# One two-block transformer kernel, one core: the first dense product begun between two halves of the transposes, and four other steps in other places

## The reference, cut to what matters

```python
# block 1
h = rmsnorm(x) ; u = h @ w_in            # ax az bq bk bv bz cq ck cv cz and gate logits
ya = pool_mixer(ax) * silu(az) ; yb = windowed_attention(bq, bk, bv) * silu(bz)
yc = causal_attention(cq, ck, cv) * silu(cz)
merged = sigmoid(g0)*(ya@wa) + sigmoid(g1)*(yb@wb) + sigmoid(g2)*(yc@wc)
x = rmsnorm(x + merged @ w_out)
# block 2
mod = silu(c) @ ada_w + ada_b            # shift1 scale1 gate1 shift2 scale2 gate2
h = rmsnorm(x)*(1+scale1) + shift1 ; proj = h @ w_in_2   # qa ka va fa qb kb vb, gates
merged = sigmoid(ga)*(forgetting_attention @ wf) + sigmoid(gb)*(stick_breaking_attention @ ws)
x = x + gate1 * (merged @ w_out_2)
y = 16 experts, top 2 of the top group   # gate, up and down matrices, 96 MB in all
x = rmsnorm(x + gate2 * y)
```

## Time and profile before

| | |
|---|---|
| runs | 710.71, 711.07, 711.32 us |
| profiled execution | 710.51 us, span 708.7 us |
| PE busy | 684.0 us (97%) |
| DVE busy | 451.4 us (64%) |
| ACT busy | 325.6 us (46%) |
| POOL busy | 2.6 us |
| DMA | 201.65 MB, mean 285 GB/s |

### The profile page before, as it was taken

One profiled execution on the slowest core, in us unless ns is written; L12 is line 12 of the kernel. 1 busy time (PEld: TensorE's weight loads), 2 busy tenths in 40 slices (PEclk: granted clock), 3 DMA queues, 4 the chain that ended last, 5 costly groups with the idle time before them and its releaser, 6 DMA issues.

```text
span 708.7 us, 9990 instructions
## 1 busy us (share of the span) xinstructions
PE 684.0 (97%) x3846; PEld 481.6 (68%) x3846; DVE 451.4 (64%) x820; ACT 325.6 (46%) x538; POOL 2.6 (0%) x5
## 2 busy tenths in 40 slices
PE   9999999999999998999999989999999999999894
PEld 4999999777788776999877658864343344343342
DVE  6578967877968888587987668675323423422425
ACT  6644444746676647333567766332213213212214
POOL 1000000000000000000000000000000000000000
PEclk9999999999999998999999999999999999999999
DMA  8977777554466432677847553687999999999961
GB/s 349 421 279 304 295 270 305 209 198 135 163 244 231 179 133 105 236 266 314 327 163 283 221 208 119 238 332 291 420 425 423 428 427 426 422 429 423 419 259 59
DMA packets 20011, 201.65 MB, mean 285 GB/s; under 512 B 2434, under 2 KB 3458, under 8 KB 7556
## 3 DMA queue, kind: packets, MB, share of 16 engines
q1 hardware_dynamic: 19248, 200.08, 71.1%
q10 hardware_dynamic: 724, 1.04, 0.5%
HBM read 200.07 MB, written 1.05 MB: 284 GB/s over the span
## 4 chain that ended last, share of the span: by engine, by line
PE 89%; ACT 3%; DMA 3%; DVE 2%; issue 2%; ACTq 0%; DVEq 0%
PE psum L911 18%; PE psum L912 17%; PE psum L913 17%; PE psum L1270 14%; PE psum L1318 8%; DMA ring<-in_expert_w_down 3%; PE psum L1235 3%; PE psum L1215 2%; PE psum L1167 2%; PE psum L1133 1%; PE psum L1113 1%; PE psum L1151 1%; ACT ring_rounded L1517 1%; DVE ring_rounded L1905 1%; PE psum L1136 1%
## 5 line engine op out<-in xcount | busy, mean ns | idle before, releaser
L1905 DVE TENSOR_TENSOR ring_rounded<-ring,ring_rounded 128x1024 fp32r<-128x1024 f32 (+1 forms) x131 | 154.2, 1212 | 29.0 <-ACT ring_rounded L1517 28.9
L1517 ACT ACTIVATE ring_rounded<-ring 128x1024 fp32r<-128x1024 f32 (+1 forms) x132 | 130.5, 1037 | 9.6 <-PE psum L913 6.8
L911 PE MATMUL psum<-hT_rounded,ring_rounded 128*128 128x256 f32 x360 | 102.5, 285 | 0.4 <-ACT foxT L1448 0.4
L913 PE MATMUL psum<-hT_rounded,ring_rounded 128*128 128x256 f32 x360 | 101.9, 283 | 0.0
L912 PE MATMUL psum<-work_rounded,ring_rounded 128*128 128x256 f32 x360 | 101.9, 283 | 0.0
L912 PE MATMUL psum<-ring_rounded,hT_rounded 128*128 128x512 f32 (+1 forms) x224 | 86.6, 386 | 0.0
L1270 PE MATMUL psum<-ring,work 128*64 128x512 f32 x320 | 83.8, 592 | 0.4 <-issue 0.4
L911 PE MATMUL psum<-ring_rounded,hT_rounded 128*128 128x512 f32 (+1 forms) x208 | 83.7, 402 | 0.0
L913 PE MATMUL psum<-ring_rounded,work_rounded 128*128 128x512 f32 (+1 forms) x208 | 80.0, 385 | 0.0
L911 PEld LDWEIGHTS psum<-hT_rounded,ring_rounded 128*128 128x128 f32 x360 | 69.1, 192 | 1.1 <-ACT foxT L1448 0.6
L912 PEld LDWEIGHTS psum<-work_rounded,ring_rounded 128*128 128x128 f32 x360 | 69.1, 192 | 0.1
(11 more groups left out here) (304 smaller groups left out, 1079.8 us busy)
## 6 DMA issues: line engine op xcount, KB each, us to landing
ring<-in_chunks SPq DMA_DIRECT2D x44, 2048.0 KB, 8.2
ring<-in_expert_w_down SPq DMA_DIRECT2D x16, 2048.0 KB, 16.2
ring<-in_expert_w_gate SPq DMA_DIRECT2D x12, 2048.0 KB, 15.1
ring<-in_expert_w_up SPq DMA_DIRECT2D x8, 2048.0 KB, 18.1
gates<-in_expert_w_up SPq DMA_DIRECT2D x8, 1024.0 KB, 21.0
hT<-in_expert_w_gate SPq DMA_DIRECT2D x4, 1024.0 KB, 15.7
mixed<-in_expert_w_gate SPq DMA_DIRECT2D x4, 1024.0 KB, 17.7
ring<-in_chunks SPq DMA_DIRECT2D x4, 512.0 KB, 7.8
```

The source lines that it names most:

```text
L911: nc.tensor.matmul(out, a[0], b[0], start=start, stop=False, skip_group_check=True)
L913: return nc.tensor.matmul(out, a[1], b[0], start=False, stop=stop, skip_group_check=True)
L1517: nc.scalar.activation(as_rounded(high_piece(c, q)), src[:, piece_of(c, q)], ACT.Copy).then_inc(chunk_hi, 1)
L1905: v.tensor_tensor(as_rounded(w[:, piece]), w[:, piece], was_rounded(high_piece(c, q)), ALU.subtract)\
```

## The change

Five groups of edits, all of them to the order of steps.

1. Start. `scale 0 1` and the last two pieces of `cv` go ahead of the second pair of `hT` units, the third piece's low part goes from POOL to DVE, and the first half of `tm cv 0` is begun on PE ahead of that pair. The `keep_busy` calls around the `hT` units fall from 2, 2, 1 and 2 to 1, 1, none and none.
2. Output product of block 1: the low parts of pieces 2 and 3 of `wout 1 1` go ahead of unit `mT 1 1 1`.
3. Second norm of block 2's input: pieces 2 and 3 of `vb` are split behind the norm steps, not ahead of them.
4. Block 2: `mod 4` and `mod 5` go from behind `FT` to right behind `fa` and `logf`; `sigmoid 0` goes from behind `tm h1 1` to behind `tm h2 0` and its heads.
5. Around `proj f`: the low part of its piece 1 goes ahead of the begin of `tm h3 1`; `gate_cols 1`, `mod 10` and `mod 11` go from around `proj s 0 0` to right behind the low parts of pieces 2 and 3, ahead of `proj f 0 0`.

```diff
@@ -50,7 +50,6 @@
 SPLIT = 4
 POOL_FROM = 4
 FIRST = ("cv",)
-FIRST_ON_POOL = 2
 ROAMING = ("va",)
 PLACED = (FIRST, ROAMING, ("proj", "b"), ("proj", "f"), ("proj", "s"), ("vb",), ("qa",), ("wout", 1, 0), ("wout", 1, 1), ("wout", 2, 1))
 PIECES = (0, 1, 2, 3)
@@ -148,15 +147,16 @@
         if low_on_dve(FIRST, q):
             steps.append(("split_low", FIRST, q))
 
-    steps += [("norm", 0, 0), ("norm", 0, 1), ("scale", 0, 0), ("scale", 0, 1)]
+    steps += [("norm", 0, 0), ("norm", 0, 1), ("scale", 0, 0)]
     split_first(0)
     unit("hT", 0, 0, 0)
     unit("hT", 0, 0, 1)
     split_first(1)
+    steps += [("begin", "tm", "cv", 0), ("scale", 0, 1)]
+    split_first(2)
+    split_first(3)
     unit("hT", 0, 1, 0)
     unit("hT", 0, 1, 1)
-    split_first(2)
-    split_first(3)
     unit("tm", "cv", 0)
     unit("tm", "cv", 1)
     for name in ("cz", "bz", "az", "ax", "cq", "ck"):
@@ -227,8 +227,8 @@
         split_placed(two, (0, 1, 2, 3), (0, 1))
         unit("wout", 1, 0, 0)
         steps.append(("norm_half", 1, 0))
+        split_placed(two, (), (2, 3))
         unit("mT", 1, 1, 1)
-        split_placed(two, (), (2, 3))
         split_placed(va, (2, 3), (0,))
         unit("wout", 1, 0, 1)
 
@@ -242,11 +242,12 @@
     unit("hT", 1, 0, 1)
     steps.append(("norm_half", 1, 1))
     split_placed(va, (), (2, 3))
-    split_placed(vb, (0, 1, 2, 3))
+    split_placed(vb, (0, 1))
     unit("wout", 1, 1, 1)
     steps.append(("norm", 1, 1))
     split_placed(vb, (), (0,))
     steps.append(("norm", 2, 1))
+    split_placed(vb, (2, 3))
 
     unit("tm", "va", 0)
     split_placed(vb, (), (1, 2, 3))
@@ -264,11 +265,11 @@
     steps.append(("gate_cols", 0))
     unit("fa",)
     steps.append(("logf",))
+    unit("mod", 4)
+    unit("mod", 5)
     unit("fm", "qb", 0)
     some_ada(2)
     unit("FT",)
-    unit("mod", 4)
-    unit("mod", 5)
     todo = pairs_of_heads(8)
     seq = [(("fm", "qb", 1), 1), (("fm", "kb", 0), 1), (("fm", "kb", 1), 2), (("tm", "h0", 0), 1),
            (("tm", "h0", 1), 2), (("tm", "h1", 0), 1), (("tm", "h1", 1), 2), (("tm", "h2", 0), 1),
@@ -279,9 +280,10 @@
         if u == ("tm", "h3", 1):
             split_placed(f, (), (0,))
             steps.append(("y_split_low", "f"))
+            split_placed(f, (), (1,))
         unit_and_heads(u, n)
         some_ada(ADA_HERE.get(u[1:], 0))
-        if u == ("tm", "h1", 1):
+        if u == ("tm", "h2", 0):
             steps.append(("sigmoid", 0))
         if u == ("tm", "h2", 1):
             steps.append(("y_split", "f"))
@@ -289,7 +291,10 @@
         if u == ("tm", "h3", 0):
             split_placed(f, (2, 3))
         if u == ("tm", "h3", 1):
-            split_placed(f, (), (1, 2, 3))
+            split_placed(f, (), (2, 3))
+            steps.append(("gate_cols", 1))
+            unit("mod", 10)
+            unit("mod", 11)
             split_placed(sb, (0, 1))
         if u == ("proj", "f", 0, 0):
             split_placed(sb, (2, 3), (0,))
@@ -300,10 +305,8 @@
             steps.append(("y_split_low", "s"))
             split_placed(sb, (), (2, 3))
     assert not todo
-    steps += [("sigmoid", 8), ("mods", 1), ("gate_cols", 1)]
+    steps += [("sigmoid", 8), ("mods", 1)]
     unit("proj", "s", 0, 0)
-    unit("mod", 10)
-    unit("mod", 11)
     unit("proj", "s", 0, 1)
     unit("mT", 2, 0, 0)
     unit("proj", "s", 1, 0)
@@ -387,7 +390,7 @@
 
 def low_on_dve(c, q):
 
-    return q != FIRST_ON_POOL if c == FIRST else q < POOL_FROM
+    return c == FIRST or q < POOL_FROM
 
 
 def chunk_of(step):
@@ -409,6 +412,7 @@
 
 STEPS, CHUNKS = plan()
 UNITS = [s[1:] for s in STEPS if s[0] == "unit"]
+BEGUN = [s[1:] for s in STEPS if s[0] == "begin"]
 SILU = ("cz", "bz", "az")
 ADA_ORDER = [s[1:] for s in STEPS if s[0] == "ada"]
 
@@ -1180,8 +1184,7 @@
                 last = nc.tensor.matmul(bank[4 + half], one_row[32 * half:32 * half + 1, :], norm_row[half],
                                         start=True, stop=True)
             last.then_inc(norm_rows_ready, 1)
-            keep_busy(2)
-            n, begun = 0, False
+            keep_busy(1)
             for s in STEPS:
                 if s[0] == "residual":
                     if s[1] == 0:
@@ -1191,15 +1194,13 @@
                     pe.wait_ge(*evicted(("wout", 2, s[1] // 2, 1)))
                     residual(s[1]).then_inc(residual_done, 1)
                 if s[0] == "begin":
-                    unit(n, s[1:], (0,))
-                    begun = True
+                    unit(UNITS.index(s[1:]), s[1:], (0,))
                 elif s[0] == "unit":
                     if s[1:] == ("rank",):
                         keep_busy_late(2, 384)
-                    unit(n, s[1:], (1,) if begun else (0, 1))
-                    n, begun = n + 1, False
-                    if s[1:] in (("hT", 0, 0, 1), ("hT", 0, 1, 0), ("hT", 0, 1, 1)):
-                        keep_busy(1 if s[3:] == (1, 0) else 2)
+                    unit(UNITS.index(s[1:]), s[1:], (1,) if s[1:] in BEGUN else (0, 1))
+                    if s[1:] == ("hT", 0, 0, 1):
+                        keep_busy(1)
                     if s[1:] == ("rank",):
                         keep_busy_late(2, 384)
                 elif s[0] == "S":
```

## The result

The changed kernel takes 712.88 us (median of 11 runs, 711.54 to 715.67), the kernel before 710.54 beside it (11 runs, 709.17 to 711.88). The ratio is 1.0034 with a 95% interval of 1.0022 to 1.0047. Forecast were 711.0, no change, with a range of 707.6 to 714.0. The time is inside the range, but the whole interval lies above 1: the change is slower, by 2.3 us where I said 0.

The account below looks back on a forecast made before the run. The prediction took PE's standing still to bound the kernel (89% of the last chain is PE). Its terms, 0.5 - 1.6 - 4.2 + 1.1 + 0 + 4.2, summed to 0.0: median 711.0 us, range 707.6 to 714.0.

Parts of the forecast that it names:

- the placing rule's move of `cz`: Start: `cz` splits land ahead of the second transposes' copies, ACT waits for the DMA, and the start loses 0.5 us.
- edits 2 and 3: Output product of block 1: -1.6 us; second norm: -1.4 us for a shorter wait and -2.8 for the clock staying up.
- `mod 4` and `mod 5` in sum: Block 2, behind `fa`: PE waits 1.55 us for `gate_cols 0` and gets 0.4 back at `FT`, +1.1 us.
- the swallowed sigmoid: `sigmoid 0` moved: PE's 1.2 us wait at V 12 goes, but the ACT and DVE chain gains nothing; worth 0.
- the wait before `mod 10`: Before `proj f`: PE stands 5 to 6 us until `gate_cols 1`, behind P 15 and the low parts, is done.
- its low clock: Behind the idle time before `mod 10` the clock falls to its lower level, +2.8 us (0 to 3.4).
- A rival: Clock falls in the 2.1 us at edit 3 or 2.0 at the start, 2.8 each; 713.8 us, chance 0.22.
- `proj f` (edit 5): Around `proj f`: T 15 comes 3.15 us later, less 1.75 for the moved mods, +1.4; low clock adds +2.8.
- The rival that priced the mods in the old waits at -1.8: At `proj f`: `gate_cols 1` comes early, mods run in the old 2.3 of waits, -1.8 for +4.2; 705.0, chance 0.07.
- -2.8 for edit 3: Second norm: with PE's wait cut from 3.50 to 2.1 us the clock stays up behind it, saving 2.8 us.

Follow-up runs that it names:

- proj_f_alone: The kernel before with edit 5 alone; 716.03 us, ratio 1.0079 to the kernel before.
- undo_proj_f: The changed kernel with edit 5 undone and the rest kept; 707.05 us, ratio 0.9953 to the kernel before.
- combo2: Kernel before plus edit 1 with `cz` pieces held back, edits 2 and 3, `sigmoid 0` moved, edit 5 with `gate_cols 1` early, `wout 2 0` placed by hand; 701.47 us.
- cols_early: The changed kernel with `gate_cols 1` moved ahead of all low parts of `proj f` and of P 15; 706.47 us, ratio 0.9948 to the kernel before.
- start_pinned: The kernel before with edit 1 and the pieces of `cz` held behind the second transposes; 709.10 us, ratio 0.9984.
- start_alone: The kernel before with edit 1 alone; 711.66 us, ratio 1.0010.

## Why the prediction was wrong

**Right, by mechanism and size.** These are the placing rule's move of `cz` (+0.57 alone for +0.5), edits 2 and 3, `mod 4` and `mod 5` in sum, the swallowed sigmoid, the wait before `mod 10` (5.79; "5 to 6 us"), its low clock. A rival named the gap lengths as what decides on the clock; see below.

**The step that failed** is in "`proj f` (edit 5)": "3.15 less the 1.75 that the mods no longer take at 433.37 is +1.4". The 1.75 did not come: that stage took +0.07. I counted PE's time as a gain without asking what DVE does in it. In the mods' old place DVE caught up with the low parts of `wout 2 0`. Two units fewer there re-spread these pieces by the very rule that I had applied to `cz` and to `qb`: each low part now stands at least one unit later in the list, and PE waits 0.54 and 1.02 for what stands behind them. I had not applied the rule to edit 5. proj_f_alone brings these waits by itself, undo_proj_f takes them away, and with the pieces placed by hand the stage takes -1.92 (combo2). This term was off by 1.82, all other terms together by -0.26, the traces' sum by 1.56. The 0.8 that the medians hold beyond that is the next step's.

The rival that priced the mods in the old waits at -1.8 had the same 1.75 in it. With `gate_cols 1` early they do run there, but V 14 to V 15 takes +0.46 and the stage behind it +0.07 (cols_early); only with the pieces by hand as well do the two stages give -1.43 (combo2).

**The step that was too sharp** is the clock's. I read two rows, the clock low behind 3.50 us and not low behind 2.0, as two sides of a bound. I also let the low stretch begin at the transposes of 272.78; it began at 272.0, while PE still stood. These are the profiled executions of all kernels here, by the gap ahead; gaps that were filled are left out:

| gap of PE | clock fell in |
|---|---|
| 1.4 to 1.6 us, at the output product, `mod 4` or `fm qb 0` | 1 of 14 |
| 2.0 us, second norm | 3 of 8 |
| 2.0 us, `proj f` | 2 of 4 |
| 3.0 us, `proj f` | 2 of 2 |
| 3.5 us, second norm | 4 of 5 |
| 4.8 and 5.8 us, before `mod 10` | 5 of 5 |

The counts are small, but in these executions a gap has a chance of a fall that grows with its length. What the rival named for the 2.0 us of edit 3 happened in 3 of 8. That -2.8 for edit 3 came out in the profiled execution was in part luck of that execution, and for the median of the runs it was likely too much. The one execution in which 3.5 us did not bring a fall, start_pinned:

```profile
270.00:272.00 2.00, 0.04 (x1) 0.07 (x2) 1.79 (x7) 0.54 (x2) 0.00 (x0) 1.00 0.03 12
272.00:274.00 2.00, 2.00 (x13) 1.81 (x14) 2.00 (x2) 1.37 (x4) 0.00 (x0) 1.00 0.00 0
274.00:276.00 2.00, 2.00 (x10) 1.66 (x9) 2.00 (x5) 2.00 (x6) 0.00 (x0) 1.00 0.03 8
```

The Trainium skill, TensorE: Matmul & The Clock Gate, section "What's actually happening", says of a kernel's start that the number of matmuls at the lower clock differs from one run to the next. These traces show such a difference in the middle of a kernel too: the clock fell behind 3.5 us in the kernel before and not in start_pinned.

What stays open: what decides, for one gap, whether the clock falls and for which of its two lengths; the missing 0.5 of start_pinned; and the 0.2 by which the mods' stage differs between executions (0.87 to 1.08).

## What to carry to other kernels

When a planner spreads work over a stretch of steps, a unit moved in or out of any stretch moves that work. So apply the rule to both ends of every move, and don't count PE's time as won at a place where another engine used it to catch up. A small instruction that others wait for is placed by what it needs, not by who comes next: `gate_cols 1` ahead of P 15 and the low parts turned +6.90 into +0.46. Price a wait of PE with its length and with the chance that the clock falls behind it, and fill it with unread matmuls where it can't be shortened.

## What the hardware showed

The clock's low stretches came in two lengths, 3.4 and 6.8 us: behind the second norm the kernel before had one of 6.8 and proj_f_alone one of 3.4, with the same order there. Where PE had no other wait, a stretch cost 0.46 to 0.48 us for each us that PE worked in it (part of it can lie in the gap itself): 2.88 for 6.0 us (kernel before), 2.56 for 5.4 (start_alone), 2.43 for 5.1 (the changed kernel, at `proj f`), 1.58 and 1.62 for 3.4 (proj_f_alone, combo2). At `proj f`, where PE also waits for low parts, one of 3.4 cost 0.95 to 1.41. The runs of the kernel before, 708.2 to 712.2 with mean clocks from 0.988 to 0.995, narrowed to 707.4 to 708.6 when the two gaps were filled.
